# Strassen's scheme in the down projections of the first three passes of an MLP, with weight sums made by adding transfers

## The chip, the core and the metric

One core of a Trainium2 chip runs the whole program. Its engines are TensorE (PE, matrix products into PSUM), VectorE (DVE), ScalarE (ACT) and GpSimd (POOL), and SyncE (SP), which here only issues transfers. The metric is the device time of one execution in microseconds (us); less is better.

## The reference

A trunk of two layers on 512 tokens of width 1024 in float32. Each layer is a mixer (attention with mLSTM in the first, SSD with RWKV-7 in the second) and an MLP; a last RMS norm follows. Only the MLP matters here:

```python
def squared_relu_mlp(h, w_up, w_down):
    return jnp.square(jax.nn.relu(h @ w_up)) @ w_down
...
    h = h + squared_relu_mlp(rmsnorm(h, mlp_norm[layer]), w_up[layer], w_down[layer])
```

`w_up` is 1024 x 4096, `w_down` 4096 x 1024.

## The kernel before

**Products.** Activations lie transposed: 128 features on the partitions, 512 tokens in the free dimension. A float32 product is made of three matmuls of rounded parts: every operand x is cut into hi (x rounded to float32r, an ACT copy) and lo (x - hi, on DVE or POOL), and a_hi b_hi + a_hi b_lo + a_lo b_hi is accumulated in PSUM.

**Passes.** The MLP of a layer runs in four passes i = 0 to 3, each over 1024 of the 4096 hidden features: an up projection to the hidden tile, the squared relu, and a down projection which is added to `h`. In pass 0 the up projection is plain: 8 tiles of 8 blocks (`plain_up`, L1220). In passes 1 to 3 it is Strassen's scheme (Winograd's form): the weight block and the activations are cut into quarters, and 7 products m1 to m7 take the place of 8. Each product is done for two halves p = 0, 1 of the output columns, so an up pass has 14 units (`UP`, `up_unit`, L1195), each of 4 blocks x 2 columns groups x 3 matmuls of 256 columns. The order of the units is m1 and m2 (both halves), then m5, m6, m3, m7, m4 of half 0, and the same of half 1. The down projection of every pass is plain: 8 tiles of 8 blocks, 192 matmuls of 512 columns (`down_part`, L1234).

**Weight units.** A unit is 512 KB of weights in one of eight places (A, B in `raw_w`; C, E in `y_mix`; 0 and 1). SP loads it once the unit before in that place is cut (L906 and following). ACT makes its hi part (`high_unit`, L1801, L1813; one 128x1024 copy), which waits until PE has done the unit four before, since there are four cut buffers. POOL makes the lo part in four quarters (`low_unit`, L1061, L1066) for pass 0, for units 12 and 13 of an up pass and for all down tiles; DVE does it in one operation (L2411, L2414) for the other units of an up pass. The scheme's four sums of weight quarters per half are made in place: two by POOL (L1069 to L1080, 128x1024), two by DVE (L2417 to L2427).

**The activations.** The products of an up unit stay in PSUM; ACT copies some of them (`copy`, L1853), DVE combines them into the hidden quarters c11, c12, c22, c21 (`quarter_of`, L2429, two operations each), ACT squares and rounds them (`hidden`, L1865), DVE makes the lo part (`low_hidden`, L2453). After each down tile DVE adds PSUM to `h` (`add`, L2458, L2460).

**Order.** Every engine runs one hand-written list of instructions in order, with waits on counters (semaphores) between engines. What is written first in an engine's list holds back all that follows on it; the lists of the MLP are `mlp` in each engine's block (L1185 PE, L1830 ACT, L2373 DVE, and the loops at the end of POOL's and SP's blocks).

Of the kernel before, what the change touches and what calls it, by code (L numbers as in the profile page):

```python
# [21 lines left out]

# [6 lines left out]
F32 = mybir.dt.float32  # L29
# [5 lines left out]
P = 128  # L35
# [267 lines left out]
U = {key: u for u, key in enumerate(UP)}  # L303
NUP = len(UP)
HT = T // 2
PLACES = ["A0", "A1", "B0", "B1", "C0", "C1", "E0", "E1"]
READS = {"m1": "A", "m2": "B", "m5": "A", "m6": "A", "m3": "E", "m7": "C", "m4": "A"}
DOWN_AT = ["B0", "E0", "C0", "A0", "B1", "E1", "C1", "A1"]
# [4 lines left out]
LOWS = [("c11", 0), ("c11", 1), ("c12", 0), ("c22", 0), ("c21", 0), ("c12", 1), ("c22", 1), ("c21", 1)]  # L313
# [3 lines left out]
DOWN_K = [0, 1, 2, 3, 6, 7, 4, 5]  # L317


PLAIN_AT = ["A0", "A1", "B0", "B1"]  # L320
# [6 lines left out]
def unit(layer, i, u):  # L327
    return layer * (2 * KT + 3 * (NUP + KT)) + (i and 2 * KT + (i - 1) * (NUP + KT)) + u


LAYER_UNITS = unit(1, 0, 0)
# [5 lines left out]

def cut_on_pool(i, u):
    return i == 0 or u >= NUP - 2


def place_name(i, u):
    if i == 0:
        return PLAIN_AT[u % 4]
    return READS[UP[u][0]] + str(UP[u][1]) if u < NUP else DOWN_AT[u - NUP]


LOADS = [(0, u, PLAIN_AT[u % 4]) for u in range(2 * KT)]
LOADS += [(1, "up", name) for name in ("A0", "C0", "E0", "A1", "B0", "C1", "E1", "B1")]
for _i in range(1, 4):  # L350
    LOADS += [(_i, NUP + j, DOWN_AT[j]) for j in range(KT)]
    if _i < 3:
        LOADS += [(_i + 1, "up", name) for name in DOWN_AT]
LOAD_COUNT = {}
_loads = {name: 0 for name in PLACES}
for _layer in range(2):
    for _i, _what, _name in LOADS:
        _loads[_name] += 1
        LOAD_COUNT[_layer, _i, _what if _what != "up" else _name] = _loads[_name]
# [3 lines left out]
for _layer in range(2):  # L363
    for _i in range(4):
        for _u in range(ups(_i) + KT):
            _on = cut_on_pool(_i, _u)
            _counts[_on] += PARTS if _on else 1
            CUT_COUNT.append((_on, _counts[_on]))
# [122 lines left out]
def trunk(nc, dram, out):  # L491
    PLAN = make_plan()
    with ExitStack() as ctx:
# [62 lines left out]
        d_parts = cut(arena, 12288, 4, HT)  # L556
# [54 lines left out]
        u_full = {name: sem(f"u_full_{name}") for name in PLACES}  # L611
# [6 lines left out]
        gained, parted, part_high, part_low = sem("gained"), sem("d_parted"), sem("part_high"), sem("part_low")  # L618

# [43 lines left out]
        def place(layer, name):  # L663
            p = int(name[1])
            if name[0] in "AB":
                r = (base["mlp", layer] + 2 * (name[0] == "B") + p) % RING
                return raw_all[:, r * KT * SW:(r + 1) * KT * SW]
            y = 2 * p + (name[0] == "E")
            return y_t[:, y * KT * SW:(y + 1) * KT * SW]
# [10 lines left out]
        def unit_cut(eng, layer, i, u, part=PARTS):  # L680

            on_pool, count = CUT_COUNT[unit(layer, i, u)]
            if on_pool:
                eng.wait_ge(u_cut_pool, count - PARTS + part)
            else:
                eng.wait_ge(u_cut_dve, count)
# [7 lines left out]
        def hid_turn(layer, i, key):  # L694

            if i == 0:
                return 32 * layer + key + 1
            return 32 * layer + 8 * i + LOWS.index(key) + 1

        def loaded(eng, layer, i, u):  # L700
            name = place_name(i, u)
            eng.wait_ge(u_full[name], 16 * LOAD_COUNT[layer, i, u if i == 0 or u >= NUP else name])

        def quarter_tile(c):

            if c in ("c11", "c12"):
# [4 lines left out]

        def quarter(hid, c, p):
            f = 4 * p + 2 * (c[2] == "2")
# [150 lines left out]
        def _(sp):  # L864
# [19 lines left out]
            def load(n, src, tile=raw_w):  # L884

                over_last = n - base["in", 1]
                if 0 <= over_last < RING:

                    unit_cut(sp, 0, 3, NUP + (3, 7, 0, 4)[over_last])
# [2303 lines left out]
```

## Time and profile before

| | us |
|---|---|
| median of three runs | 1301.35 (1301.01 to 1302.15) |
| the profiled execution: its own time | 1299.8 |
| the profiled execution: span from first to last instruction | 1298.0 |
| PE busy in the span | 1255.2 |
| DVE, ACT, POOL busy | 739.0, 616.1, 594.9 |

The time of the execution is 1.8 us more than its span. Matmuls are pipelined, and a matmul's listed duration is longer than the step from one start to the next, so a stage is read by the starts. Layer 0's MLP runs from 251.65 to about 593 us of the span, layer 1's from about 944 to 1287 us.

### The profile page before, as it was taken

How to read it: one execution, taken by the hardware profiler on the slowest of the kernel's cores; microseconds unless marked ns; L12 is line 12 of the kernel's file. 1: busy time of each engine (PE TensorE's matmuls, PEld its weight loads, DVE VectorE, ACT ScalarE, POOL GpSimd, SP SyncE). 2: the span in 40 equal slices, each digit the busy share in tenths (PEclk: the TensorE clock that was granted, in tenths of full speed). 3: DMA queues.
4: the chain of work that ended last, by engine and by line, in shares of the span. 5: the costliest groups of instructions: out<-in, count | busy, mean ns of one | idle time of the engine just before them, and what ended most of it. 6: DMA issues, size and time to landing. Idle time of an engine off the chain costs nothing.

```text
span 1298.0 us, 19296 instructions
## 1 busy us (share of the span) xinstructions
PE 1255.2 (97%) x7549; PEld 1057.7 (81%) x7549; DVE 739.0 (57%) x1099; ACT 616.1 (47%) x990; POOL 594.9 (46%) x689
## 2 busy tenths in 40 slices
PE   6999978999999999999999999999999999999997
PEld 5777756788998988988777778888888898998986
DVE  4438665572562734743789975476554373562743
ACT  5335674463362542734582634753554263361641
POOL 4653224756256083373445543312656426265080
PEclk9999998999999999999999999999999999999999
DMA  9322101336153251422222321000334335152311
GB/s 283 95 74 71 61 17 33 101 94 174 45 151 87 82 148 32 131 68 63 71 61 65 97 66 49 2 2 1 98 102 111 112 116 143 47 142 74 97 34 65
DMA packets 173482, 109.18 MB, mean 84 GB/s; under 512 B 4570, under 2 KB 170704, under 8 KB 173392
## 3 DMA queue, kind: packets, MB, share of 16 engines
q1 hardware_dynamic: 172976, 107.88, 29.2%
q8 instruction: 61, 1.00, 0.3%
q14 instruction: 29, 0.24, 0.1%
q0 software_dynamic: 416, 0.07, 0.0%
HBM read 105.83 MB, written 2.10 MB: 83 GB/s over the span
## 4 chain that ended last, share of the span: by engine, by line
PE 86%; DVE 8%; ACT 3%; issue 2%; DMA 1%; SPq 0%; DVEq 0%; ACTq 0%
PE ps L1251 9%; PE ps L1252 9%; PE ps L1253 9%; PE ps L1217 6%; PE ps L1216 6%; PE ps L1215 6%; PE ps L1120 6%; PE ps L1121 5%; PE ps L1122 5%; PE ps L1107 3%; PE ps L1229 2%; PE ps L1230 2%; PE ps L1231 2%; PE ps L1594 1%; PE ps L1170 1%
## 5 line engine op out<-in xcount | busy, mean ns | idle before, releaser
L998 POOL TENSOR_TENSOR w_lo<-raw_w,w_hi 128x256 fp32r<-128x256 f32 x248 | 213.0, 890 | 266.8 <-ACT w_hi L1747 266.8
L2460 DVE TENSOR_TENSOR h<-h,ps 128x512 f32<-128x512 f32 x64 | 44.0, 687 | 211.2 <-PE ps L1253 211.2
L1120 PE MATMUL ps<-hn_hi,w_hi 128*128 128x512 f32 x368 | 153.1, 416 | 2.5 <-POOL w_lo L998 2.4
L1121 PE MATMUL ps<-hn_lo,w_hi 128*128 128x512 f32 x368 | 146.6, 398 | 0.0
L1122 PE MATMUL ps<-hn_hi,w_lo 128*128 128x512 f32 x368 | 146.6, 398 | 0.0
L1066 POOL TENSOR_TENSOR wx_lo<-raw_w,wx_hi 128x256 fp32r<-128x256 f32 x128 | 98.1, 800 | 40.1 <-ACT wx_hi L1813 40.1
L1813 ACT ACTIVATE wx_hi<-raw_w 128x1024 fp32r<-128x1024 f32 x62 | 65.4, 1054 | 104.1 <-PE ps L1253 91.6
L1066 POOL TENSOR_TENSOR wx_lo<-y_mix,wx_hi 128x256 fp32r<-128x256 f32 x64 | 51.8, 842 | 137.4 <-ACT wx_hi L1813 137.4
L1813 ACT ACTIVATE w_hi<-raw_w 128x1024 fp32r<-128x1024 f32 x54 | 57.0, 1055 | 113.1 <-PE ps L1253 102.9
L1066 POOL TENSOR_TENSOR w_lo<-raw_w,w_hi 128x256 fp32r<-128x256 f32 x120 | 90.0, 783 | 42.8 <-ACT w_hi L1813 42.8
L1251 PE MATMUL ps<-hid_hi,w_hi 128*128 128x512 f32 x256 | 101.1, 395 | 0.0
L1252 PE MATMUL ps<-hid_lo,w_hi 128*128 128x512 f32 x256 | 101.1, 395 | 0.0
L1253 PE MATMUL ps<-hid_hi,w_lo 128*128 128x512 f32 x256 | 101.0, 395 | 0.0
L1252 PE MATMUL ps<-hid_lo,wx_hi 128*128 128x512 f32 x256 | 100.6, 393 | 0.0
L1251 PE MATMUL ps<-hid_hi,wx_hi 128*128 128x512 f32 x256 | 100.5, 393 | 0.0
L1253 PE MATMUL ps<-hid_hi,wx_lo 128*128 128x512 f32 x256 | 99.6, 389 | 0.0
L1747 ACT ACTIVATE w_hi<-raw_w 128x1024 fp32r<-128x1024 f32 x62 | 65.3, 1054 | 52.8 <-issue 51.4
L1120 PEld LDWEIGHTS ps<-hn_hi,w_hi 128*128 128x128 f32 x368 | 69.9, 190 | 23.5 <-issue 6.8
L1121 PEld LDWEIGHTS ps<-hn_lo,w_hi 128*128 128x128 f32 x368 | 69.8, 190 | 17.7 <-issue 2.4
L1122 PEld LDWEIGHTS ps<-hn_hi,w_lo 128*128 128x128 f32 x368 | 69.8, 190 | 17.1
L1066 POOL TENSOR_TENSOR w_lo<-y_mix,w_hi 128x256 fp32r<-128x256 f32 x56 | 45.1, 840 | 69.7 <-ACT w_hi L1813 69.7
L1215 PE MATMUL ps<-hn_hi,wx_hi 128*128 128x256 f32 x208 | 58.0, 279 | 0.0
(477 smaller groups left out, 3347.8 us busy)
## 6 DMA issues: line engine op xcount, KB each, us to landing
raw_w<-in_w_up SPq DMA_DIRECT2D x40, 512.0 KB, 4.2
raw_w<-in_w_down SPq DMA_DIRECT2D x40, 512.0 KB, 4.1
raw_w<-in_o_w_in SPq DMA_DIRECT2D x27, 512.0 KB, 3.7
y_mix<-in_w_up SPq DMA_DIRECT2D x24, 512.0 KB, 4.6
y_mix<-in_w_down SPq DMA_DIRECT2D x24, 512.0 KB, 4.5
raw_w<-in_e_w_in SPq DMA_DIRECT2D x19, 512.0 KB, 3.7
raw_w<-in_e_w_out SPq DMA_DIRECT2D x8, 512.0 KB, 3.5
raw_w<-in_o_w_out SPq DMA_DIRECT2D x8, 512.0 KB, 3.7
```

Of the source, the lines that this page charges most:

```text
L998: nc.gpsimd.tensor_tensor(w_lo[:, n % CUT, ks], raw_w[:, n % RING, ks], w_hi[:, n % CUT, ks].bitcast(F32), ALU.subtract).then_inc(w_cut, 1)
L1066: nc.gpsimd.tensor_tensor(lo_[:, c], raw_[:, c], hi_[:, c].bitcast(F32), ALU.subtract).then_inc(u_cut_pool, 1)
L1120: mm(o, a_hi, b_hi, start=(k == 0), stop=False)
L1121: mm(o, a_hi, b_lo, start=False, stop=False)
L1122: ins = mm(o, a_lo, b_hi, start=False, stop=(k == KT - 1))
L1215: mm(om, a_hi, x_hi, start=opens, stop=False, skip_group_check=True)
L1216: mm(om, a_hi, x_lo, start=False, stop=False, skip_group_check=True)
L1217: ins = mm(om, a_lo, x_hi, start=False, stop=(k == 3), skip_group_check=True)
L1251: mm(o, hi_[:, k, :], hid_hi[:, k, :], start=(k == 0), stop=False, skip_group_check=True)
L1252: mm(o, hi_[:, k, :], hid_lo[:, k, :], start=False, stop=False, skip_group_check=True)
L1253: ins = mm(o, lo_[:, k, :], hid_hi[:, k, :], start=False, stop=(k == ks[-1]), skip_group_check=True)
L1813: A(cut_buffers(layer, i, u)[0], place(layer, place_name(i, u)), ACT.Copy).then_inc(u_high, 1)
```

## The change

In passes 0 to 2 of both layers the down projection is done by the same scheme as the up projection: 7 products, 14 units of 256 columns, with the hidden quarters as the moving operand. Pass 0's up projection and pass 3's down projection stay plain.

- **Order of the down units (PE):** m1, m2, m5, m6, m3, m7, m4, half 0 and half 1 of each in turn (`DN`).
- **Weights:** quarters A, B, C and G are loaded. The sums A+C, C+E and A+C+E, A+C+E+B (in G) are made by transfers that POOL issues and that add to what lies in the place (`add_load`, `accum_op=ALU.add`): ten a pass. B's place is loaded a second time with E.
- **Cuts:** nine of the fourteen units on POOL, now in two halves of 512 columns, five (the second halves of m5, m6, m3, m7, m4) on DVE. The up units 12 and 13 on POOL are cut in two halves too.
- **Operands:** the hidden quarters are kept as they are (`kept`), squared only. DVE forms four differences or sums in place (`form`), ACT rounds the operand of each product (`operand_high`), DVE makes its lo part (`operand_low`), seven of each a pass, in three buffers in turn. The per-quarter rounding of `hidden` and `low_hidden` is left in pass 3 alone.
- **Results:** DVE adds or subtracts each unit's PSUM result to one or two quarters of `h` (`fold`), 16 operations of 512 elements a pass, in the place of the 8 of `add`.
- The places of the weights change from pass to pass (`UP_AT`, `DOWN_AT`), and so do a few waits at the layers' borders.

The core of the diff, in the order tables, SP's later loads of a pass, POOL, PE, ACT, and DVE's list for a down pass:

```diff
+PRODUCTS = ["m1", "m2", "m5", "m6", "m3", "m7", "m4"]
+DN = [(q, p) for q in PRODUCTS for p in range(2)]
+DOWN_READS = {"m1": "A", "m2": "B", "m5": "A", "m6": "G", "m3": "B", "m7": "C", "m4": "G"}
 def cut_on_pool(i, u):
+    if u >= ups(i):
+        return i == 3 or u - ups(i) not in (5, 7, 9, 11, 13)
     return i == 0 or u >= NUP - 2
+SOURCE = {"A": (0, 0), "B": (1, 0), "C": (0, 1), "E": (1, 1), "G": (0, 0)}
+ADDED = {"A": ["C"], "C": ["E"], "G": ["C", "E", "B"]}
...
+                        for p in range(2):
+                            unit_cut(sp, layer, i, dnu(i, "m2", p))
+                            load_down(i, f"B{p}", 1)
+                        for name, q in (("A", "m5"), ("B", "m3"), ("C", "m7"), ("E", "m4")):
+                            for p in range(2):
+                                unit_cut(sp, layer, i, dnu(i, q, p))
+                                load_up(i + 1, f"{name}{p}")
...
+                def add_load(i, name, n):
+                    at = down_at(i, name)
+                    if name[0] == "A":
+                        unit_cut(pool, layer, i, dnu(i, "m1", int(name[1])))
+                    elif n == 0:
+                        is_loaded(pool, at, layer, i, "down", name, 0)
+                    elif n == 1:
+                        is_added(pool, layer, i, name, 0)
+                    else:
+                        unit_cut(pool, layer, i, dnu(i, "m6", int(name[1])))
+                    pool.dma_start(quarters_of(place(layer, at)),
+                                   down_quarter(layer, i, ADDED[name[0]][n], int(name[1])), accum_op=ALU.add
+                                   ).then_inc(u_added[at], 16)
...
+                for i in range(4):
+                    if i == 0:
+                        for u in range(6):
+                            low_unit(0, u)
+                        add_load(0, "G0", 0)
+                        low_unit(0, 6)
+                        low_unit(0, 7)
+                        add_load(0, "G0", 1)
+                    else:
+                        for p in range(2):
+                            sum_first(i, p)
+                            sum_third(i, p)
+                        if i < 3:
+                            add_load(i, "G0", 0)
+                            add_load(i, "C0", 0)
+                            add_load(i, "G0", 1)
+                        low_unit(i, NUP - 2)
+                        low_unit(i, NUP - 1)
...
+                    low_unit(i, dnu(i, "m1", 0))
+                    add_load(i, "A0", 0)
+                    low_unit(i, dnu(i, "m1", 1))
+                    add_load(i, "A1", 0)
+                    if i == 0:
+                        add_load(i, "C0", 0)
+                    add_load(i, "G1", 0)
+                    low_unit(i, dnu(i, "m2", 0))
+                    if i:
+                        add_load(i, "C1", 0)
+                    low_unit(i, dnu(i, "m2", 1))
+                    low_unit(i, dnu(i, "m5", 0))
+                    add_load(i, "G1", 1)
+                    low_unit(i, dnu(i, "m6", 0))
+                    if i == 0:
+                        add_load(i, "C1", 0)
+                    add_load(i, "G0", 2)
+                    add_load(i, "G1", 2)
+                    low_unit(i, dnu(i, "m3", 0))
+                    low_unit(i, dnu(i, "m7", 0))
+                    low_unit(i, dnu(i, "m4", 0))
...
+                def down_product(i, q, p):
+                    folded_first = {"m6": "a1", "m3": "z5", "m7": "x6", "m4": "b1"}
...
+                        if k == 0 and p == 0:
+                            pe.wait_ge(op_low, 7 * (3 * layer + i) + PRODUCTS.index(q) + 1)
...
+                    if i < 3:
+                        first = ups(i)
+                        for n, q in ((3, None), (4, "m5"), (6, "m6"), (8, "m3"), (10, "m7"), (12, "m4")):
+                            if n > 3:
+                                high_unit(layer, i, first + n)
+                                high_unit(layer, i, first + n + 1)
+                            elif i == 0:
+                                high_unit(layer, 0, first + 3)
+                                third_high()
+                            if q:
+                                operand_high(i, q)
...
+                    form(i, "d3")
+                    form(i, "d1")
+                    fold(i, "a1", 0)
+                    operand_low(i, "m5")
+                    if i == 0:
+                        third_low()
+                    fold(i, "a1", 1)
+                    form(i, "d2")
+                    low_unit(i, dnu(i, "m5", 1))
+                    fold(i, "b1", 0)
+                    operand_low(i, "m6")
+                    fold(i, "b1", 1)
+                    form(i, "d4")
+                    low_unit(i, dnu(i, "m6", 1))
+                    fold(i, "z5", 0)
+                    operand_low(i, "m3")
+                    fold(i, "z5", 1)
+                    low_unit(i, dnu(i, "m3", 1))
...
+                    low_unit(i + 1, 3)
```

## Rows read from the trace of the kernel before

**Rows 1.** the page: the span, busy time and its share, the chain's shares by engine

```profile
span 1298.0 us, 19296 instructions
PE 1255.2 (97%) x7549; PEld 1057.7 (81%) x7549; DVE 739.0 (57%) x1099; ACT 616.1 (47%) x990; POOL 594.9 (46%) x689
PE 86%; DVE 8%; ACT 3%; issue 2%; DMA 1%; SPq 0%; DVEq 0%; ACTq 0%
```

**Rows 2.** busy time by stage, layer 0: up 1, down 1, up 2, down 2

```profile
core 0: us, PE busy (x) PEld busy (x) DVE busy (x) ACT busy (x) POOL busy (x), PEclk, DMA share, GB/s
341.30:380.80 39.50, 39.50 (x337) 39.50 (x336) 28.74 (x34) 26.20 (x35) 9.76 (x14) 1.00 0.38 108
380.80:425.10 44.30, 44.30 (x194) 36.00 (x193) 13.23 (x15) 10.47 (x12) 29.40 (x31) 1.00 0.36 95
425.10:464.60 39.50, 39.50 (x338) 39.45 (x337) 28.74 (x34) 26.21 (x35) 9.73 (x14) 1.00 0.37 108
464.60:508.90 44.30, 44.30 (x194) 35.97 (x193) 13.36 (x15) 10.48 (x12) 29.37 (x31) 1.00 0.36 95
```

**Rows 3.** timeline of PE: start us, us; the ends of down pass 1

```profile
380.83 0.40 PE L1251 MATMUL ps<-hid_hi,w_hi 128*128 128x512 f32 x1
425.21 0.28 PE L1215 MATMUL ps<-hn_hi,w_hi 128*128 128x256 f32 x1
```

**Rows 4.** timeline of POOL: cuts of units 12, 13, 15 and 17

```profile
370.20 2.83 POOL L1066 TENSOR_TENSOR wx_lo<-y_mix,wx_hi 128x256 fp32r<-128x256 f32 x4 [32.33 <-ACT wx_hi L1813]
373.87 2.84 POOL L1066 TENSOR_TENSOR wx_lo<-raw_w,wx_hi 128x256 fp32r<-128x256 f32 x4 [0.84 <-ACT wx_hi L1813]
379.45 3.31 POOL L1066 TENSOR_TENSOR w_lo<-y_mix,w_hi 128x256 fp32r<-128x256 f32 x4
386.48 2.83 POOL L1066 TENSOR_TENSOR wx_lo<-raw_w,wx_hi 128x256 fp32r<-128x256 f32 x4
```

**Rows 5.** groups of POOL by line: busy us, mean ns of one

```profile
L1050 POOL TENSOR_TENSOR rwkv_raw<-rwkv_raw,y_mix 128x512 f32<-128x512 f32 x4 | 5.1, 1272 | 0.3
L1074 POOL TENSOR_TENSOR raw_w<-raw_w,y_mix 128x1024 f32<-128x1024 f32 x12 | 28.9, 2405 | 30.7 <-DVE wx_lo L2414 20.3 <-DVE w_lo L2414 10.3
```

**Rows 6.** timelines of POOL's sums and of DVE in down pass 1

```profile
411.22 2.40 POOL L1074 TENSOR_TENSOR raw_w<-raw_w,y_mix 128x1024 f32<-128x1024 f32 x1 [4.01 <-DVE w_lo L2414]
419.51 2.41 POOL L1080 TENSOR_TENSOR y_mix<-y_mix 128x1024 f32<-128x1024 f32 x1
389.43 0.69 DVE L2460 TENSOR_TENSOR h<-h,ps 128x512 f32<-128x512 f32 x1 [4.20 <-PE ps L1253]
409.91 1.23 DVE L2414 TENSOR_TENSOR w_lo<-raw_w,w_hi 128x1024 fp32r<-128x1024 f32 x1 [0.41 <-ACT w_hi L1813]
421.00 2.00 DVE L2414 TENSOR_TENSOR wx_lo<-raw_w,wx_hi 128x1024 fp32r<-128x1024 f32 x1 [0.40 <-ACT wx_hi L1813]
```

**Rows 7.** timeline of ACT: a square, a copy of a unit

```profile
380.36 0.63 ACT L1869 ACTIVATE arena<-arena 128x512 f32<-128x512 f32 x1 [0.61 <-DVE arena L2450]
408.82 1.06 ACT L1813 ACTIVATE w_hi<-raw_w 128x1024 fp32r<-128x1024 f32 x1 [4.54 <-PE ps L1253]
```

**Rows 8.** POOL's issues (timeline); transfers: KB each, median us from issue to landing

```profile
3.58 0.51 POOL L989 DMA_DIRECT2D arena<-in_ml_conv_b  x1
4.08 0.54 POOL L989 DMA_DIRECT2D arena<-in_ssm_conv_w  x1
arena<-in_mix_norm POOLq DMA_DIRECT2D x1, 8.0 KB, 3.8
arena<-in_ssm_conv_w POOLq DMA_DIRECT2D x1, 16.0 KB, 5.0
raw_w<-in_w_down SPq DMA_DIRECT2D x40, 512.0 KB, 4.1
main<-in_main_const SPq DMA_DIRECT2D x1, 66.0 KB, 1.9
```

More of the change, by code:

```diff
@@ L23 @@
+import math
 from contextlib import ExitStack
@@ L316, with downs @@
 SUM_OF = {"m5": "t1", "m6": "t2", "m7": "t3", "m4": "t4"}
-DOWN_K = [0, 1, 2, 3, 6, 7, 4, 5]
-PLAIN_AT = ["A0", "A1", "B0", "B1"]
+FORMED = ["d3", "d1", "d2", "d4"]
+FOLDS = [(f, p) for f in ("a1", "b1", "z5", "x6", "z3") for p in range(2)]
+FOLDS += [("x7", 0), ("y7", 0), ("x7", 1), ("y7", 1), ("v4", 0), ("v4", 1)]
+DOWN_FIRST, DOWN_OTHER = [0, 1, 4, 5], [6, 7, 2, 3]
 def ups(i):
     return NUP if i else KT
+def downs(i):
+    return KT if i == 3 else NUP
 def unit(layer, i, u):
-    return layer * (2 * KT + 3 * (NUP + KT)) + (i and 2 * KT + (i - 1) * (NUP + KT)) + u
@@ L331, with dnu, in_halves @@
-LAYER_UNITS = unit(1, 0, 0)
+    return layer * 100 + sum(ups(n) + downs(n) for n in range(i)) + u
+assert unit(0, 4, 0) == 100
+def dnu(i, q, p):
+    return ups(i) + DN.index((q, p))
 def pass_index(layer, i):
     return 3 * layer + i - 1
+def in_halves(i, u):
+    return (i > 0 and u < NUP) or (i < 3 and u >= ups(i))
 def cut_on_pool(i, u):
+    if u >= ups(i):
+        return i == 3 or u - ups(i) not in (5, 7, 9, 11, 13)
     return i == 0 or u >= NUP - 2
[L342 to L345, printed above, removed]
@@ L348, with _places @@
[L348 to L355, printed above, removed]
-for _layer in range(2):
-    for _i, _what, _name in LOADS:
-        _loads[_name] += 1
-        LOAD_COUNT[_layer, _i, _what if _what != "up" else _name] = _loads[_name]
+def _places():
+    at = {"A": (0, 1), "B": (2, 3), "C": (6, 7), "G": (4, 5)}
+    up, down = {}, {0: at}
+    for i in range(1, 4):
+        up[i] = {"A": at["A"], "B": at["B"], "C": at["C"], "E": at["G"]}
+        at = {"A": up[i]["B"], "B": up[i]["C"], "C": up[i]["A"], "G": up[i]["E"]}
+        down[i] = at
+    return up, down
@@ L678, in cut_buffers, with unit_cut @@
             return hi[:, s], lo[:, s]
-        def unit_cut(eng, layer, i, u, part=PARTS):
-            on_pool, count = CUT_COUNT[unit(layer, i, u)]
+        def unit_cut(eng, layer, i, u, share=1.0):
+            on_pool, count, parts = CUT_COUNT[unit(layer, i, u)]
             if on_pool:
-                eng.wait_ge(u_cut_pool, count - PARTS + part)
+                eng.wait_ge(u_cut_pool, count - parts + math.ceil(parts * share))
             else:
@@ L1831, in mlp @@
                 n0 = base["mlp", layer]
+                gains, parts, third = (place(layer, n) for n in (6, 5, 7))
                 def hidden_whole(j):
[L1834 to L1838 removed]
+                    act.wait_ge(relued, hid_turn(layer, 0, j))
+                    A(kept_tile(j), kept_tile(j), ACT.Square).then_inc(hid_square, 1)
                 def gain_pair(pair):
```

712 lines of the change are left out of this document (434 added, 278 removed).

## The prediction, made before the change was built

> **What bounds the kernel now.** I read the page first: TensorE (PE) is busy 97% of the span and holds 86% of the chain that ended last [rows 1]. So the question is which stretches are wholly PE's, and that is the table by stage: in the up passes and down passes of layer 0 PE is busy for the whole of each stretch at the full clock (39.50 of 39.50 us, 44.30 of 44.30), while DVE, ACT and POOL have room [rows 2]. The reader is to see that the two kinds of stage differ: in an up pass (already Strassen) DVE is busy 28.7 us and POOL 9.7; in a down pass DVE 13.2 and POOL 29.4. Layer 1 shows the same stretches. The other views are read for prices: the timelines of POOL, DVE and ACT round one border between up and down [rows 3 to 7] and the list of transfers [rows 8].
>
> **What the change removes from PE.** A plain down pass is 8 tiles x 8 blocks x 3 matmuls = 192 of 512 columns; the new one is 14 units x 24 = 336 of 256 columns, the shape, count and operands' types of an up pass. The plain pass takes 44.4 us (380.83 to 425.21) [rows 3] and the up pass 39.5 [rows 2], so 4.9 us go per pass if PE never waits; six passes (three in each of two layers): 29.4 us. One unit is 39.5 / 14 = 2.82 us. That is half of a plain tile's 5.55, and this is what matters for the rest: cuts and sums must now come twice as often.
>
> **What is added beside PE.** With all operands in SBUF, one DVE operation on 128x1024 takes 1.23 us alone, but 2.00 us where POOL was in a sum that began 1.49 us earlier and ended 0.92 us into it; 2.00 less 0.92 is 1.08, so DVE did nothing until POOL ended [rows 6]. I therefore count such DVE operations and POOL's as excluding each other; a DVE operation with a PSUM input (0.69 us) is outside this count. Per up and down pass together, after the change: POOL has 4 sums x 2.40 and 11 units in two halves of 1.27 [rows 5], 37.5 us; DVE has 17 units, 4 sums, 7 operand parts and 4 formed operands, 32 x 1.23 = 39.4 us. Together 77 of PE's 79 us. DVE's 16 folds and 16 quarter operations (0.69 each, 22 us) and POOL's ten adding transfers come on top, but outside the exclusion. So the cover is nearly used up, on average; what is lost is decided where several of these meet in one queue.
>
> **The place: the start of the down pass, POOL's queue.** Time 0 is PE's first matmul of the pass (380.83). In the trace POOL starts the cut of up unit 12 at -10.6, with a gap of 0.84 us before the next, and goes on without a pause to the end of unit 17 at +8.5 [rows 4]. After the change the queue from the same start is units 12, 13, m1 (two), m2 (two), m5's first, and between them the adds A0, A1, G1 and C1. In passes 1 and 2: -10.6 + 0.84 + 7 x 2.54 = 8.0. The adds' issue: POOL's small transfers hold it 0.51 us (4 rows) and 0.54 (32 rows) [rows 8]; an add has 512 rows of 1 KB. Bounds 0.5 (no growth) and 1.1 (0.03 / 28 us a row, carried on); I take 0.8, 3.2 us for four: 11.2. Exclusion: the halves of the last three units meet DVE's operand parts of m2 and m5 and the first two formed operands, four x 1.23 = 4.9 at worst, 0 at best; I take 2.0: 13.2.
>
> Only then does POOL issue the second addition to G1, the weight sum of m6's second half; it waits for the first addition to land, which was issued about 8 us before. Landing: no adding transfer is in the trace. Lower bound 4.1 us, the plain 512 KB from SP's queue; POOL's own queue takes 3.8 us from issue to landing for 8 KB (5.0 for 16 KB), SP's 1.9 for 66 KB and 4.1 for 512, so the bytes cost about 2.2 [rows 8]. 3.8 + 2.2 = 6.0 is a plain load through POOL's queue, and I take it; if the second read of an add costs as much again, 5.0 + 4.4 = 9.4, the upper bound. So it lands at 19.2.
>
> The Trainium skill, DMA: Bandwidth & Descriptors, section Anatomy of one DMA (SWDGE path), gives about 2.0 us plus bytes over 436 GB/s, for 512 KB an estimate of 3.2 us. The row for 8 KB is already above it; by the page the sum below would come to -7.6 instead of +7.6.
>
> **Who waits.** ACT's order is the copy of m6's first half, of its second half, and then the rounded operand of m6. So both halves of m6 stand behind that landing: copy 1.06, operand 1.06 [rows 7], DVE's low part 1.23, hand-overs 0.1: 3.4 us, 22.6. PE would want m6 after six units, at 16.9. Stall 5.7 us. Behind m6's operand DVE has a fold, the fourth formed operand and the cut of m6's second half: 0.69 + 2 x 1.23 = 3.2 against PE's 2.82, and more if POOL is in between: 0.3 to 1.5, I take 0.7. The later products have two such DVE operations and two folds each (3.8 us of 5.6), so they catch up. m5's operand stands in the same way behind the add to A1 (issued near 2, landed near 8, operand ready near 11.5 against 11.2); its wait lies inside m6's.
>
> **The border to the next up pass.** POOL's four sums lay inside the down pass (411.22 on), where DVE had pauses [rows 6]. Now C and E are loaded only as m7 and m4 are cut, so the sums slide to the first ten us of the up pass, 2.40 each in DVE's way while DVE cuts units of 2.82. From 0 (the pauses hide them) to 4 us; I take 1.0.
>
> **Pass 0.** Its up tiles last 5.55 us, so POOL isn't behind. The cut of m2's second half waits for ACT: last relu 0.69, square 0.63, operand of m2 1.06, copy 1.06 = 3.4 [rows 6, 7]; then two units of POOL, 8.5, exclusion 1.0, issue at 9.5, landing 15.5, m6's operand at 18.9: stall 2.0.
>
> **Nothing else on the path.** ACT's eight roundings of the activations (0.63 each) go, and a down pass holds 14 copies and 5 operand parts (19 x 1.06 = 20 of 39 us): covered by ACT's own pauses. Loads by SP: 18 of 512 KB per down and next up, as against 16, besides the adds; no wait for SP's is late in the walk. Pass 3, the borders of the layers and the end keep their plain tiles; other buffers come free last at a layer's border, hidden by tile 7's 5.55 us: 0.
>
> **The sum.** Passes 1 and 2 of both layers: 5.7 + 0.7 + 1.0 - 4.9 = +2.5, four times: +10.0. Pass 0, twice: 2.0 + 0.7 + 1.0 - 4.9 = -1.2: -2.4. Together +7.6 on the profiled execution's 1299.8 us: 1307.4; the median of the runs is 1.55 higher (1301.35): **1309**.
>
> **Rivals.** *The adds land in time.* Issue 0.5, no exclusion at this place, landing 4.1: in passes 1 and 2 the stall is 10.0 + 4.1 + 3.4 - 16.9 = 0.6 and in pass 0 none: 4 x -4.3 + 2 x -4.9 = -27, 1274; with half of the way to my values about 1291. It decides at a landing of about 4 to 5 us from issue. For it: the DMA share is only 0.36 in these stages [rows 2]; against it: POOL's queue needs 3.8 us for 8 KB. The page's 3.2 us lies on this side. I put the case at 1274 to 1297, **0.36**. *My case*, the G1 landing and its followers at 1304 to 1322: **0.40**. *The exclusion is the bound*: DVE and POOL have 77 us that exclude each other and meet badly all along, with waits of 4.9 at m6, 1.5 behind it and 4.0 at the border: 4 x (8.6 + 1.5 + 4.0 - 4.9) + 2 x (3.4 + 1.5 + 4.0 - 4.9) = +45, 1346; half way from mine 1328. For it: 77 of 79; against it: each engine alone has 15 us to spare per pair of passes. 1322 to 1346, **0.14**. *Loss and gain cancel*, 1298.7 to 1304: **0.10**. That the shorter matmuls don't deliver their half is excluded by the up passes [rows 2].
>
> What no row shows: a DVE operation beside POOL's writing of descriptors. The Trainium skill, SBUF (State Buffer), section Who interferes with whom, infers that a tensor-tensor of DVE takes only the shared read side, which descriptor writing doesn't need; if that is wrong, four issues wait up to 1.23 each, which is inside the third case.
>
> **How the numbers follow.** A measurement of this kernel tells 0.2% (2.6 us) from no change. Faster 0.36, same 0.10, slower 0.54. The range takes in the first rival but for its last 2 us and half of the third, 1276 to 1334; the likeliest case alone is 1304 to 1322.
>
> **What would show it.** Right: PE's busy sum in a down pass near 39.5, with one idle time of 4 to 8 us before m6 in passes 1 and 2, smaller in pass 0, ended by DVE's operand part behind ACT behind an adding transfer; POOL's add to G1 issued 11 to 16 us into the pass and 5 to 9 us to its landing. Wrong: no idle time before m6 (first rival), or many idle times of under 2 us behind cuts by POOL and DVE, with DVE's 128x1024 operations at a mean over 1.6 us (third).

## The result, and the profile after

The changed kernel takes 1374.39 us (median of 4 runs, 1373.17 to 1375.33) where the kernel before, measured beside it, takes 1301.18 (1300.85 to 1302.15): a ratio of 1.056, 95% interval 1.054 to 1.058. It is 73 us slower. I had forecast slower, but by 8 us, and the time lies outside my range of 1276 to 1334. The profiled execution is the one of 1374.36 us.

First the page of after, to be held against [rows 1]: the span, the busy times, the shares of the chain that ended last, one group of DVE, POOL's adding transfers as instructions, and the same transfers from issue to landing (KB, median us).

```profile
span 1372.6 us, 21256 instructions
PE 1266.5 (92%) x8413; PEld 1112.5 (81%) x8413; DVE 974.3 (71%) x1195; ACT 660.2 (48%) x1020; POOL 690.3 (50%) x641
PE 60%; DVE 26%; issue 6%; ACT 5%; DMA 2%; POOL 1%; SPq 0%; DVEq 0%; ACTq 0%
...
L2689 DVE TENSOR_TENSOR hid_lo<-arena,hid_hi 128x1024 fp32r<-128x1024 f32 x36 | 99.5, 2763 | 35.0 <-ACT hid_hi L2086 35.0
L1208 POOL DMA_DIRECT2D y_mix<-in_w_down x44 | 68.0, 1591 | 104.7 <-DMA y_mix<-in_w_down 70.4
...
y_mix<-in_w_down POOLq DMA_DIRECT2D x44, 512.0 KB, 8.3
```

PE's share of the chain has gone from 86% to 60%, and DVE's from 8% to 26%, though DVE is busy only 71% of the span. The stages of layer 0 say where (same columns as [rows 2]): down pass 0, down pass 1, up pass 2.

```profile
core 0: us, PE busy (x) PEld busy (x) DVE busy (x) ACT busy (x) POOL busy (x), PEclk, DMA share, GB/s
298.67:351.70 53.03, 44.80 (x338) 44.45 (x337) 45.24 (x34) 22.11 (x22) 29.87 (x22) 0.87 0.83 184
391.65:448.74 57.09, 46.83 (x339) 45.93 (x338) 49.00 (x35) 20.61 (x21) 33.62 (x25) 0.88 0.76 159
448.74:488.64 39.90, 39.88 (x338) 39.70 (x337) 32.90 (x31) 23.41 (x31) 20.84 (x13) 1.00 0.58 144
```

The up pass is nearly as it was (39.90 us instead of 39.50, PE busy throughout). The down pass, 44.30 us before and in my forecast 39.5 without a wait and 45.9 with its waits (5.7 and 0.7), takes 57.09, and in it PE is idle for 10 us *and* has a granted clock of 0.88 of full speed. From the starts of the fourteen units in PE's timeline, the six down passes last 334.0 us, against 6 x 39.5 = 237 without a wait: 65.8 us are idle time ahead of a unit, 30.9 us are units that took longer than 2.71 us, most of them 4 to 5 us. With 5 us more in the six up passes and 29 us of forecast gain, that is the 73.

Who ended the idle time (the list of PE's waits in the MLP stages: us in total, times, the longest):

```profile
engine line waited for: us in total, times, longest us
PE ps L1368 <- DVE hid_lo L2689: 49.9, 12, 5.1
PE ps L1368 <- issue: 7.3, 4, 2.0
PE ps L1368 <- DVE hid_lo L2686: 2.9, 3, 2.5
```

L2689 is DVE's low part of every operand but m6's, L2686 that of m6. So PE stands before m2, m5 and m3 (2 to 5 us each; 19.8, 18.1 and 24.5 of the 65.8 us), and hardly before m6 (3.4 us), where I had put the stall. Before m5, before m3 and, in pass 0, before m2 it waits for DVE. Before m2 in passes 1 and 2 (the four waits of the row "issue") it starts 0.1 us after the record of the first piece of POOL's cut of m2 ends.

The place itself, down pass 1 (it starts at 391.65): DVE's timeline, then POOL's (start us, us).

```profile
396.18 10.61 DVE L2704 TENSOR_TENSOR arena<-arena 128x1024 f32<-128x1024 f32 x2
...
396.26 1.84 POOL L1208 DMA_DIRECT2D y_mix<-in_w_down  x1
397.03 3.58 POOL L1181 TENSOR_TENSOR w_lo<-y_mix,w_hi 128x512 fp32r<-128x512 f32 x2
399.69 2.19 POOL L1208 DMA_DIRECT2D raw_w<-in_w_down  x1
400.51 3.93 POOL L1181 TENSOR_TENSOR w_lo<-y_mix,w_hi 128x512 fp32r<-128x512 f32 x2
402.99 4.91 POOL L1181 TENSOR_TENSOR wx_lo<-raw_w,wx_hi 128x512 fp32r<-128x512 f32 x2
405.47 3.69 POOL L1208 DMA_DIRECT2D y_mix<-in_w_down  x1
```

Two formed operands, 1.22 us each when DVE is alone, take 10.61 us: the second began at 397.42 and ended at 406.79. Less its own 1.2 us it got in at about 405.5, where POOL's run of cuts ended and the next issue began. That is not one POOL operation in the way but six pieces with an issue among them. The minimum, median and maximum (ns) of this line, and of the low parts, say the same: most are undisturbed, four of the first are held for eight to nine microseconds and eight of the second for five to seven.

```profile
L2704 DVE TENSOR_TENSOR arena<-arena x24: 1210/1224/10562, 309.2 to 1245.7; 128x1024 f32<-128x1024 f32 x24
L2689 DVE TENSOR_TENSOR hid_lo<-arena,hid_hi x36: 1209/1226/7890, 293.9 to 1265.3; 128x1024 fp32r<-128x1024 f32 x36
```

The largest of the three waits, m3's, is not at the start of the pass. There POOL stands idle for 9.34 us until DVE has cut m6's second half, then issues the third addition to G1 and starts the cuts of m3, m7 and m4 without a pause, just ahead of DVE's low part for m3 (POOL's timeline, then DVE's).

```profile
422.63 1.28 POOL L1208 DMA_DIRECT2D y_mix<-in_w_down  x1 [9.34 <-DVE w_lo L2635]
423.40 3.08 POOL L1181 TENSOR_TENSOR wx_lo<-y_mix,wx_hi 128x512 fp32r<-128x512 f32 x2
425.92 3.01 POOL L1181 TENSOR_TENSOR w_lo<-raw_w,w_hi 128x512 fp32r<-128x512 f32 x2
...
422.78 7.25 DVE L2689 TENSOR_TENSOR hid_lo<-arena,hid_hi 128x1024 fp32r<-128x1024 f32 x1
```

And what a wait of PE costs beyond itself, PE's timeline at m2's first half: 2.02 us idle, then matmuls that start every 0.21 us until 402.61, and every 0.12 from there. The window 399.30 to 402.60 has a granted clock of 0.52, the lower of the two levels.

```profile
399.49 0.55 PE L1368 MATMUL ps<-hid_hi,w_hi 128*128 128x256 f32 x1 [2.02 <-issue]
399.84 0.41 PE L1369 MATMUL ps<-hid_lo,w_hi 128*128 128x256 f32 x1
...
402.61 0.39 PE L1370 MATMUL ps<-hid_hi,w_lo 128*128 128x256 f32 x1
402.83 0.29 PE L1368 MATMUL ps<-hid_hi,w_hi 128*128 128x256 f32 x1
402.96 0.28 PE L1369 MATMUL ps<-hid_lo,w_hi 128*128 128x256 f32 x1
```

### The profile page after: what moved, and what is told of

Its sections match the earlier page's. It is cut to its first block, busy times and chain, and to the rows that moved or that the text cites. A ratio compares the mean times of both kernels' runs of the same rounds, so it can differ in the third digit from the quotient of the medians.

```text
span 1372.6 us, 21256 instructions
## 1 busy us (share of the span) xinstructions
PE 1266.5 (92%) x8413; PEld 1112.5 (81%) x8413; DVE 974.3 (71%) x1195; ACT 660.2 (48%) x1020; POOL 690.3 (50%) x641
## 4 chain that ended last, share of the span: by engine, by line
PE 60%; DVE 26%; issue 6%; ACT 5%; DMA 2%; POOL 1%; SPq 0%; DVEq 0%; ACTq 0%
PE ps L1368 5%; PE ps L1284 5%; PE ps L1285 5%; PE ps L1286 5%; DVE hid_lo L2689 5%; PE ps L1369 5%; PE ps L1370 5%; DVE arena L2704 3%; DVE wx_lo L2635 3%; PE ps L1271 3%; DVE w_lo L2635 2%; PE ps L1435 2%; PE ps L1417 2%; PE ps L1418 2%; PE ps L1436 2%
## 5 line engine op out<-in xcount | busy, mean ns | idle before, releaser
L1111 POOL TENSOR_TENSOR w_lo<-raw_w,w_hi 128x256 fp32r<-128x256 f32 x248 | 214.4, 896 | 265.7 <-ACT w_hi L1930 265.7
L1368 PE MATMUL ps<-hid_hi,wx_hi 128*128 128x256 f32 x384 | 118.1, 308 | 40.5 <-DVE hid_lo L2689 40.4
L1181 POOL TENSOR_TENSOR w_lo<-raw_w,w_hi 128x256 fp32r<-128x256 f32 (+1 forms) x88 | 97.5, 1273 | 62.3 <-ACT w_hi L2007 62.3
L2689 DVE TENSOR_TENSOR hid_lo<-arena,hid_hi 128x1024 fp32r<-128x1024 f32 x36 | 99.5, 2763 | 35.0 <-ACT hid_hi L2086 35.0
L1208 POOL DMA_DIRECT2D y_mix<-in_w_down x44 | 68.0, 1591 | 104.7 <-DMA y_mix<-in_w_down 70.4
L1369 PE MATMUL ps<-hid_lo,wx_hi 128*128 128x256 f32 x384 | 116.6, 304 | 0.0
L1370 PE MATMUL ps<-hid_hi,wx_lo 128*128 128x256 f32 x384 | 116.5, 303 | 0.0
L1368 PE MATMUL ps<-hid_hi,w_hi 128*128 128x256 f32 x288 | 86.1, 299 | 21.4 <-DVE hid_lo L2689 9.5
L1181 POOL TENSOR_TENSOR wx_lo<-raw_w,wx_hi 128x256 fp32r<-128x256 f32 (+1 forms) x80 | 89.7, 1245 | 14.4 <-ACT wx_hi L2007 14.4
L1370 PE MATMUL ps<-hid_hi,w_lo 128*128 128x256 f32 x288 | 84.7, 294 | 0.0
L1369 PE MATMUL ps<-hid_lo,w_hi 128*128 128x256 f32 x288 | 84.7, 294 | 0.0
```

The costliest lines, as they stand in the source:

```text
L1111: nc.gpsimd.tensor_tensor(w_lo[:, n % CUT, ks], raw_w[:, n % RING, ks], w_hi[:, n % CUT, ks].bitcast(F32), ALU.subtract).then_inc(w_cut, 1)
L1181: nc.gpsimd.tensor_tensor(lo_[:, c], raw_[:, c], hi_[:, c].bitcast(F32), ALU.subtract).then_inc(u_cut_pool, 1)
L1208: pool.dma_start(quarters_of(place(layer, at)), down_quarter(layer, i, ADDED[name[0]][n], int(name[1])), accum_op=ALU.add).then_inc(u_adde ...
L1368: mm(om, a_hi, x_hi, start=(opens and k == 0 and m == 0), stop=False, skip_group_check=True)
L1369: mm(om, a_hi, x_lo, start=False, stop=False, skip_group_check=True)
L1370: ins = mm(om, a_lo, x_hi, start=False, stop=(k == 3), skip_group_check=True)
```

## The experiments

Two theories. **E**: DVE's operations on two SBUF inputs are held up by POOL's cuts, and what counts is how they meet. **L**: the adding transfers are longer than I took (8.3 us from issue to landing, and an issue recorded at 1.3 to 1.8 us), so the operands that stand behind them are late. All runs in one table; every time is set against the kernel before as measured beside it (1307.92 us for quarters, eighths, plain_adds and quarters_plain; 1299.49 for short_cuts, short_cuts_plain, paced and adds_first; 1299.86 for dve_short, first_short, paced_plain and dve_short_plain; 1301.32 for the last two). Each row but the first and the last is one run, and the four runs of the last spread over 19 us, so a difference of a few microseconds tells nothing. The 1307.92 is 5 to 9 us above the other times of the kernel before, which makes the four rows set against it look some 7 us better; the column of the six down passes does not depend on it. "Idle" and "slow units" are PE's in the six down passes, from the starts of its units; a slow unit is one of over 2.71 us, at the lower clock or, in paced above all, waiting for the second piece of a cut. "DVE held" is what DVE's operations on SBUF alone took beyond their length alone, summed over the MLP stages, with the longest; against the shortest operation of the same line and shape the sums come out 16 to 28 us lower in every row, the changed kernel's at 156.

| kernel | us over before | six down passes | idle | slow units | DVE held (longest) |
|---|---|---|---|---|---|
| the changed kernel | +73.2 | 334.0 | 65.8 | 30.9 | 178 (9.3) |
| quarters | +76.0 | 338.8 | 75.4 | 27.1 | 136 (7.4) |
| eighths | +96.2 | 341.1 | 71.3 | 32.5 | 156 (9.3) |
| plain_adds | +36.5 | 303.8 | 47.9 | 19.0 | 146 (5.4) |
| quarters_plain | +43.5 | 309.6 | 41.7 | 30.7 | 115 (5.8) |
| short_cuts | +32.7 | 288.0 | 41.5 | 9.5 | 73 (2.2) |
| short_cuts_plain | -19.9 | 239.2 | 1.6 | 0.2 | 73 (2.2) |
| paced | +92.2 | 347.3 | 81.2 | 29.7 | 138 (3.0) |
| adds_first | +59.9 | 309.2 | 56.7 | 21.8 | 166 (6.9) |
| dve_short | +44.0 | 300.3 | 49.3 | 14.7 | 137 (7.0) |
| first_short | +11.5 | 261.0 | 23.4 | 3.3 | 73 (2.2) |
| paced_plain | +44.0 | 303.2 | 45.1 | 21.4 | 124 (2.2) |
| dve_short_plain | +10.3 | 266.5 | 21.3 | 8.0 | 133 (5.7) |
| early_dve | +76.4 | 336.7 | 76.8 | 22.7 | 117 (6.0) |
| early_dve_first | +52.1 | 306.1 | 56.0 | 18.4 | 127 (5.9) |

In the kernel before, DVE is held 44 us in all (22 by the other count), never over 0.8. No kernel that does the whole work beats it.

**Narrower pieces: quarters and eighths.** POOL's cuts of a unit in four or eight pieces instead of two.

```
-_parts = 1 if not _on else 2 if in_halves(_i, _u) else PARTS
+_parts = 1 if not _on else PARTS        # quarters; 8 for in_halves in eighths
```

> One size changed: POOL cuts its units in four pieces of 256 columns again instead of two of 512. Theory E (while POOL works off pieces of 512 columns back to back, a DVE operation with two SBUF inputs does not get in until the run ends, up to 9.3 us in the changed kernel's trace; beside pieces of 256 columns it waited 0.8 us at most in the kernel before): DVE's waits fall from 178 us in all to under 70, PE's idle times before m2, m5 and m3 go but for those that are left behind the adding transfers, 1295 to 1325 us. Theory L (the adding transfers, 8.3 us from issue to landing, and their place in POOL's queue bound the down passes): POOL becomes a little slower, 1370 to 1385 us.

> POOL cuts its units of 256-column products in eight pieces of 128 columns. Theory E in the form that a piece's width decides whether DVE gets in between two pieces: as good as four pieces or better for DVE's waits, but POOL's unit is dearer by its fixed part (about 8 x 0.15 us more than two pieces), 1300 to 1335. If only the total of POOL's and DVE's work counted, it would be slower than two pieces, over 1375.

Measured 1383.9 and 1404.1 us. If DVE waited for the running piece only, narrower pieces would have freed it; the longest waits stayed at 7.4 and 9.3 us, so DVE waits through several pieces, however wide. E in the form "DVE waits for one piece", on which my forecast rested, falls. The times lie where theory L had put the one (1370 to 1385) and the mere total of the work the other (over 1375). In quarters half of PE's idle time, 36 of 75 us, is now before m6.

**Transfers without the addition: plain_adds and quarters_plain.**

```
-down_quarter(layer, i, ADDED[name[0]][n], int(name[1])), accum_op=ALU.add
+down_quarter(layer, i, ADDED[name[0]][n], int(name[1]))
```

> The ten transfers that POOL issues in a pass overwrite instead of adding, so the weight sums of the down passes are left out; issue, queue, bytes and waits stay. Theory L: landing falls from 8.3 us towards 6, and with it the time by 2 us for each pass or more, 1340 to 1362. Theory E: the runs of 512-column pieces are as long as before, 1366 to 1378.

> Both: pieces of 256 columns, and transfers that overwrite (the weight sums of the down passes are left out). With theory E the landing matters only now: 5 to 20 us below the run with pieces of 256 columns alone, 1280 to 1310. With theory L alone it equals the run with overwriting transfers, 1340 to 1365.

1344.45 and 1351.42 us, both in the range of theory L: 30 of the 97 us that the down passes lost go with the addition (37 by the first column), and narrower pieces don't help here either. The transfers' own rows in plain_adds (POOL's instruction: minimum, median, maximum in ns; then issue to landing) are to be read against 1591 ns and 8.3 us above.

```profile
L1208 POOL DMA_DIRECT2D y_mix<-in_w_down x42: 748/766/798, 294.1 to 1218.9; - x42
...
y_mix<-in_w_down POOLq DMA_DIRECT2D x44, 512.0 KB, 5.5
```

So L has a large part. But the longest hold of DVE is still 5.4 us, and PE stands idle 48 us.

**Cuts taken away: short_cuts and short_cuts_plain.**

```
-c = slice(q * w, (q + 1) * w)
+c = slice(q * w, q * w + 64) if in_halves(i, u) else slice(q * w, (q + 1) * w)
```

> Each of POOL's cuts in halves covers only 64 of its 512 columns, so most of the low parts of those units are left out; the adding transfers and their places stay. The changed kernel stands 73 us above the kernel before. Theory E (the waits of VectorE behind POOL's back-to-back cuts are most of the loss): VectorE's waits fall from 178 us to under 60, PE's idle times before m2 and m5 go, and the kernel comes to 10 to 30 us above the kernel before, what is left being the landing of the adds at m6. Theory L (the adding transfers by themselves, 8.3 us from issue to landing, are most of the loss): the queue is shorter but each landing is as long; 45 us or more above the kernel before, PE waiting at m6 and m4.

> POOL's cuts shortened to 64 columns as in the run before and its transfers overwriting instead of adding, so most low parts and the weight sums by transfers are left out. If E and L together are the whole loss, PE works through its units of 2.7 to 2.8 us with hardly an idle time: 15 to 30 us below the kernel before (the 29 us that I forecast as the gain). If the time stays within 10 us of the kernel before, a third cause is at work (VectorE's own work, the border of the passes, or the loads).

1332.16 us, 33 over the kernel before and so between my two readings, and 1279.62, 20 under it as I had put it. With both causes away the down pass is what I had worked out: 39.57 us, PE busy throughout, at full clock (same columns as [rows 2]).

```profile
377.55:417.12 39.57, 39.57 (x338) 39.57 (x337) 31.93 (x34) 20.46 (x21) 15.51 (x18) 1.00 0.71 215
```

With the adding transfers alone (short_cuts) nearly all of PE's waiting is at one place, m6, six times:

```profile
PE ps L1368 <- DVE hid_lo L2686: 34.6, 6, 7.7
PE ps L1368 <- DVE hid_lo L2689: 4.9, 4, 2.1
```

From the units' starts it is 7.0 to 7.9 us in passes 1 and 2 and 2.3 to 3.2 in pass 0, where my forecast had 5.7 and 2.0. The place is the one I had put; the way to it in passes 1 and 2 is not. There was no queue of cuts to hold the second addition to G1 back: POOL stood idle 4.7 to 6.2 us ahead of it until the first had landed, which took 11.1 to 12.9 us (pass 1 of layer 0):

```profile
397.03 1.30 POOL L1208 DMA_DIRECT2D y_mix<-in_w_down  x1 [6.25 <-DMA y_mix<-in_w_down]
```

DVE's formed operands in the same kernel are undisturbed, though all 60 adding transfers are issued:

```profile
L2704 DVE TENSOR_TENSOR arena<-arena x24: 1218/1222/1346, 302.3 to 1208.1; 128x1024 f32<-128x1024 f32 x24
```

The four corners don't add up: by the six down passes the cuts alone give back 46 us, the addition alone 30, both 95 (40, 37 and 93 by the first column). Where one of the two makes an operand late, the other's lateness lies beside it.

**A pause between the pieces: paced, and paced_plain.** Every piece waits until POOL's own piece before is complete.

```
+if in_halves(i, u):
+    pool.wait_ge(u_cut_pool, CUT_COUNT[unit(layer, i, u)][1] - parts + q)
 nc.gpsimd.tensor_tensor(lo_[:, c], raw_[:, c], hi_[:, c].bitcast(F32), ALU.subtract
```

> All the work is done; each of POOL's cuts in halves waits for POOL's own piece before to be complete, so that there is a pause between two pieces. If VectorE is kept out because back-to-back pieces leave no pause (theory E in its second form, since narrower pieces did not help), its waits of 5 to 10 us go, none is over 2.5 us, their sum falls from 178 to under 90 us and the kernel comes to 30 to 50 us above the kernel before. If the pause makes no difference (what keeps VectorE out is something else, the writing of descriptors for example), it stays 65 to 80 us above.

> Each of POOL's cuts in halves waits for its own piece before, and the transfers overwrite instead of adding (the weight sums by transfers are left out). With adding transfers the pause took VectorE's longest wait from 9 to 3 us and still made the kernel 18 us slower than the changed one, PE waiting at m6. If that is because the later cuts push the additions back, then with cheap transfers the pause gains: 20 to 35 us above the kernel before, where plain transfers without the pause were 36.5 above theirs. If the lengthened queue of cuts itself is late for PE, it is 45 us or more above.

In paced the longest hold falls from 9.3 to 3.0 us, near what theory E's second form wanted, though their sum, 138 us, stays far above its 90, and the line of the low parts, up to 7.9 us in the changed kernel, stays under 3.6:

```profile
L2691 DVE TENSOR_TENSOR hid_lo<-arena,hid_hi x36: 1224/1826/3559, 292.1 to 1282.2; 128x1024 fp32r<-128x1024 f32 x36
```

The time is 1391.71 us all the same, 92 over, slower than either reading had it. Now POOL waits for DVE where DVE waited for POOL, its cuts end later, the additions behind them are issued later, and PE's list shows the price at m6 (L2688 there): 10.7 to 11.1 us in each of passes 1 and 2.

```profile
PE ps L1370 <- DVE hid_lo L2688: 56.8, 6, 10.9
```

With plain transfers the pause gives 44 us over before, at the border of what I had set for the two readings and no better than plain_adds without it (36.5). Who waits for whom can be turned round; the work on two SBUF inputs stays the same.

**The other side's work: dve_short and dve_short_plain.** DVE's seven operand parts and four formed operands cover 256 of 1024 columns, POOL's work is whole.

```
-V.tensor_tensor(kept[dst], kept[x], kept[y], op)
+V.tensor_tensor(kept[dst][:, 0:1, :], kept[x][:, 0:1, :], kept[y][:, 0:1, :], op)
```

> The seven low parts of the activations' operands and the four formed operands of each down pass cover 256 of their 1024 columns on VectorE (11 operations of about 0.4 us instead of 1.23), so most of those low parts and three quarters of the formed operands are left out; POOL's cuts and adding transfers are whole. It shortens VectorE's use of the shared side, not its waiting, and leaves POOL's queue as long as it was. If the loss of theory E is VectorE's waiting behind POOL, the single waits of 5 to 9 us stay and the kernel stays 50 us or more above the kernel before. If it is the amount of work that excludes each other, VectorE's 9 us a pass count like POOL's (whose 20 us a pass gave 40): 45 us or less above it.

> VectorE's 11 operations of a down pass shortened as in the first of these runs and the transfers overwriting (low parts, formed operands and weight sums by transfers left out). Plain transfers alone stood 36.5 us above the kernel before, with POOL's cuts shortened as well 20 below. If VectorE's work counts like POOL's, -5 to +15; if only POOL's uninterrupted runs matter, +20 to +35.

1343.84 and 1310.15 us. Some 9 us less of DVE's work a pass gives back 34 us of the down passes and, with plain transfers, 37 (29 and 26 by the first column). The single holds stay at 7.0 and 5.7 us, as the theory of mere waiting said, but the gain is that of the theory of the amount: both engines' work counts, not only POOL's runs. These edits shorten an engine's own list along with the excluded work. That DVE's list in the down passes is not too long by itself is shown by short_cuts_plain, where it is whole and PE is idle for 1.6 us; for POOL's list no run separates the two.

**The order of the additions: adds_first and first_short.** In passes 1 and 2 G1's first addition goes ahead of m1's cuts, its second ahead of C1's and of the last cuts of m2 and m5.

```
 low_unit(i, NUP - 1)
+if i < 3:
+    add_load(i, "G1", 0)
...
 low_unit(i, dnu(i, "m2", 0))
 if i:
+    add_load(i, "G1", 1)
     add_load(i, "C1", 0)
```

> All the work is done; in passes 1 and 2 the first addition to G1 is issued ahead of m1's cuts and the second ahead of C1's and of the last cuts of m2 and m5, some 4 to 6 us earlier. Theory L at m6 (my forecast's mechanism): m6's second half starts earlier and 10 to 25 us go (48 to 63 above the kernel before). Theory E: the waits before m2, m5 and m3 stay, PE waits there instead, and it stays 65 to 80 us above.

> POOL's cuts in halves shortened to 64 columns (most of the low parts left out) and in passes 1 and 2 G1's two additions moved ahead in POOL's queue, both edits of runs before together. With the short cuts alone PE stood 7.2 to 8.0 us before m6 in passes 1 and 2 and the kernel was 33 us above the kernel before. If the place of G1's additions in the queue makes that stall, it falls to under 4 us and the kernel comes to 5 to 20 us above. If it is the two landings in a row, whatever their place, it stays over 6 us and 25 us or more above.

1359.36 us, 13 less than the changed kernel's distance, with all the work done; m6's stall is gone and m5, m2 and m3 still wait (31 us behind DVE's low parts). m6 had only 3.4 us to give: the gain is at m3 (24.5 to 11.2 us of idle time) and m5 (18.1 to 12.1), while m1 and m2 lose 14 us. With short cuts it is 1311.33 us and m6's stall falls in passes 1 and 2 from 7.0 to 7.9 us to between 0 and 1.4. So the place of the additions in POOL's queue was a lever at m6, though, with short cuts, by their own landings and not by the cuts ahead of them.

**Less of the excluded work in the first units: early_dve and early_dve_first.** From POOL's cut of m1's second half, about the start of the pass, to PE's m5, four units of 2.82 us later, POOL has four cuts (m1, m2 twice, m5) and DVE two operand parts and two formed operands, all on SBUF alone: 4 x 2.5 + 4 x 1.23 = 14.9 us, due in some 10.8. DVE does a cut in half the time, so m2's two halves and m5's first were moved to it: 11.1 us.

```
-return i == 3 or u - ups(i) not in (5, 7, 9, 11, 13)
+return i == 3 or u - ups(i) not in (2, 3, 4, 5, 7, 9, 11, 13)
...
 operand_low(i, "m2")
+low_unit(i, dnu(i, "m2", 0))
 form(i, "d3")
 form(i, "d1")
+low_unit(i, dnu(i, "m2", 1))
 fold(i, "a1", 0)
 operand_low(i, "m5")
+low_unit(i, dnu(i, "m5", 0))
```

> All the work is done; the cuts of m2's two halves and of m5's first half go from POOL (two pieces, 2.5 us) to DVE (one operation, 1.23 us) ahead of the operations that DVE has there; the additions follow each other in POOL's queue without cuts between them. If the amount of work that excludes each other at the start of the pass is what costs (14.9 us due in 10.8 us, now 11.1), PE's idle times before m2, m5 and m3 shrink to 1 us or less, G1's second addition is issued as its first has landed, and the kernel comes to 5 to 35 us above the kernel before, with what is left at m6. If DVE becomes late by its own work (it has 65 of 79 us by my count), PE waits for DVE operations that took 1.2 us each, and it stays 40 us or more above.

> The same three cuts on DVE, and in passes 1 and 2 G1's first addition ahead of m1's cuts, so that the second can be issued some 4 us earlier. With the cuts shortened this order took the stall before m6 from 7.5 to about 1 us and the time from 33 to 11.5 us above the kernel before. If both causes are named rightly: 0 to 20 us above it (below it only if hardly any wait is left). If POOL's runs as such are what holds DVE up, or DVE's own work, 25 us or more above.

early_dve takes 1377.67 us, not the 5 to 35 over before that I had expected. In passes 1 and 2 the idle time before m2 is all but gone (0.5 to 0.7 us are left at its second half) and 1.7 to 1.9 are left before m5, but m3 still waits 2.7 to 3.5 us and m6 now 9.1 to 9.7. The chain of waits of this kernel between 395 and 418 us shows nothing but the two additions to G1, one behind the other (start us, us):

```profile
395.99 11.38 DMA y_mix<-in_w_down
407.38 0.28 issue
407.66 9.33 DMA y_mix<-in_w_down
...
417.07 0.04 ACT w_hi L2004
```

POOL's queue holds no cut between the two; it issues the second 0.28 us after the first has landed. Issued within 1.6 us of two other additions, the first takes 11.4 us instead of the median 8.3. So with the cuts out of the way the two landings are the whole stall at m6, as in short_cuts. early_dve_first, with G1 ahead, takes 1353.38 us (1346.79 to 1365.54; ratio 1.042, 1.035 to 1.049), with adds_first the fastest of those that do all the work and still 52 over before: m6 no longer waits, but the addition to A0 is now behind G1's, and PE waits 3.0 to 6.5 us before m5 for a cut that stands behind its landing, and in three of those four passes 2.9 to 3.8 us before m3. My expectation of 0 to 20 failed there: each addition that is moved ahead moves another back, and each takes 5.4 to 18.2 us from issue to landing, 8.4 in the median.

## Why the prediction was wrong

**Right.** The gain without a wait: 44.30 to 39.57 us a pass in short_cuts_plain. That the start of the down pass and POOL's queue decide, in part: 24.5 of the 65.8 us of idle time are at m3, further on. The queue walk: the second addition to G1 was put at 13.2 us into pass 1, and is issued at 405.47 - 391.65 = 13.8. The issue of an addition, taken at 0.8 us: the next instruction of POOL starts 0.8 us behind it (396.26 to 397.03). The border: 1.0 us a pass, measured 5 in six. In part luck: the stall before m6, 5.7 us in passes 1 and 2 and 2.0 in pass 0, against 7.0 to 7.9 and 2.3 to 3.2 in short_cuts; in passes 1 and 2 two landings in a row made it there, not the queue of cuts that I had walked through. That DVE's operations don't suffer from the writing of descriptors: short_cuts, 1222 ns as the median and 1346 at most beside 60 adding transfers. The Trainium skill, SBUF — State Buffer, section Who interferes with whom, infers this, and the run agrees.

**The step that failed is the exclusion's term**, "four x 1.23 = 4.9 at worst, 0 at best; I take 2.0". It rested on one row [rows 6], in which DVE waited for the one sum that was running, and so it priced a meeting at DVE's own length. And it stood in POOL's queue alone, as what POOL loses to DVE; what DVE loses behind POOL was put at nothing. In the changed kernel the first or second formed operand of passes 1 and 2 is held for 8.2 to 9.3 us, through a whole run of cuts, and DVE is held 178 us in all instead of 44. So m5's operand, put at 11.5 us into the pass with a wait "inside m6's", was ready at 17.5 to 19.5, and m3's wait, which had no term, is the largest. The Trainium skill, SBUF — State Buffer, section Summary: rules for kernel authors, says that where DVE has two SBUF inputs and the GpSimd operation reads SBUF, the second to issue blocks until the first finishes; by that a wait would end with the running piece of 1.3 us. The measurement decides here: it went through up to six pieces and the issues between them. I had seen the total (77 us of 79) and given its case 0.14, because an average leaves room. It should have been summed where it is due: 14.9 us in the first 10.8 of a pass. That would have stood against the chance of my own case before any run.

**The landing was mis-sized**, 6.0 us taken and 9.4 as the bound; the median is 8.3, and the one in the sum, G1's second addition, took 10.6 to 10.8 us in passes 1 and 2 (5.7 in pass 0). Of my two terms the plain load through POOL's queue was near (5.5 in plain_adds against 6.0); the addition costs 2.8 us on top in the median. Its issue is recorded longer (0.77 us plain, 1.59 on average adding), but the next instruction starts as soon behind it. An estimate by the Trainium skill, DMA: Bandwidth & Descriptors, section Anatomy of one DMA (SWDGE path), gave 3.2 us; neither kind of transfer here is that short.

**A term that I did not have** is the clock: in the changed kernel each of the fifteen waits of 2 to 5 us before a unit of the down passes is followed by a unit of 4.3 to 5.0 us instead of 2.71, and the slow units make 30.9 us over the six passes. Not every wait costs this: in short_cuts one of 3.2 us before m6 is followed by a unit of 2.78, and its idle time of 41.5 us has 9.5 us of slow units beside it. In [rows 2] the clock stands at 1.00 everywhere, and PE never waits there; a forecast that puts PE to waiting has to have a term for it.

**The rivals.** The third, the exclusion as the bound, has the mechanism, and its sign in the trace is there: DVE's low parts at a mean of 2763 ns, where I had named 1600. Its waits come to 74 us, against 66 measured and 5 at the borders, but it had them at m6 and the border, and no clock in its price of 45 us. The first, additions that land in time, is excluded: the landing that it wanted at 4 to 5 us took 10.6 to 10.8, and with POOL's cuts shortened the additions still leave the kernel 33 us over before. My own case is a real cause, but in the changed kernel PE is already late at m2 and m5 by the time it would show at m6 (0 to 2.6 us).

**The sum, set right.** Six down passes at 334.0 instead of 266 us are +68, and the up passes +5: 73. By the runs, of the 95 us of the down passes between the changed kernel and short_cuts_plain, 46 go with POOL's cuts alone, 30 with the addition alone, and 19 only when both are away.

## What to carry to other kernels

When two engines exclude each other, add up the excluded work between two due times, not over a stage: 77 of 79 us seemed just to fit, and 14.9 in 10.8 could not. A weight sum made by a transfer is not free because no engine's busy time shows it: here each takes 5.5 to 13 us from issue to landing, a second one to the same place comes on top of that, and moving one ahead moves another back. And price a stall of PE with the slow matmuls that can follow it: in the changed kernel half of the idle time came on top, in short_cuts a quarter.

## What the runs showed of the hardware that I had not expected

- DVE with two SBUF inputs usually gets in at the end of POOL's running piece or of one further piece, even when the next is ready: in the ten of these kernels with neither a pause nor short cuts that was so in all but 2 of some 1500 meetings in unbroken runs of POOL's work without a transfer's issue in them. Where an issue stood in the run it went past three or more pieces 44 to 50 times in some 300 to 500, by how the runs are told apart, with holds of up to 9.3 us. With a pause before each piece (paced) or pieces of 64 columns (short_cuts) it never passed more than one. Why an issue makes this difference was not settled; two of the long waits (eighths, 8.9 us each) had no issue ahead of them.
- Behind an adding transfer's issue POOL's cuts overlap in the record: 1.8 us each at a pitch of 1.25, growing to 2.4 and more with each further addition; behind a plain one they take 1.3 at the same pitch. By the pitch the cuts are no slower there.
- Adding 512 KB through POOL's queue takes 8.3 us from issue to landing in the median (5.5 to 13.0), the plain load through the same queue 5.5 (plain_adds), and 11.4 was measured for an addition issued within 1.6 us of two others.
